# Gate/up expert by expert in a mixture-of-experts layer: split signals, split refills, earlier weight loads

## What is computed

```python
def hierarchical_moe(x, w_rg, b_rg, w_re, b_re, w_gate, w_up, w_down):
    ...  # gates: (tokens, 32), two nonzero entries in a row
    def per_seq(args):
        xi, gi = args
        hid = jax.nn.silu(jnp.einsum('sd,edf->sef', xi, w_gate)) * jnp.einsum('sd,edf->sef', xi, w_up)
        return jnp.einsum('sef,se,efd->sd', hid, gi, w_down)
...
x = x + jnp.concatenate([y_ssm, y_att], axis=-1) @ w_out[l]
x = x + hierarchical_moe(rmsnorm(x, norm_ffn_w[l]), ...)   # w_gate, w_up: (32, 1024, 256), w_down: (32, 256, 1024)
```

## Time and profile before

| | us |
|---|---|
| median of 3 runs | 785.33 (783.24 to 787.1) |
| the profiled execution, its own time | 782.43 |
| its span in the profile | 780.8 |
| TensorE busy | 712.0 (91%) |
| mean DMA rate over the span | 192 GB/s |
| granted TensorE clock, mean | 0.958 of full speed |

### The profile page before, as it was taken

How to read it: one execution, slowest core, us unless ns; L and a number is a source line. 1 busy time by engine, 2 the same in 40 slices (tenths; PEclk the granted TensorE clock), 3 DMA queues, 4 the chain that set the end, 5 groups by cost and what they waited for, 6 DMA issues and landing times.

```text
span 780.8 us, 10344 instructions
## 1 busy us (share of the span) xinstructions
PE 712.0 (91%) x3818; PEld 473.9 (61%) x3818; DVE 378.6 (48%) x758; ACT 279.1 (36%) x647; POOL 145.4 (19%) x124
## 2 busy tenths in 40 slices
PE   5999999999999999999999999978999678788884
PEld 4877888788788888566566688863333223233321
DVE  6776877775877734666776543660211111111100
ACT  4844643544554454544654423211221111111200
POOL 3423332330320102001210132011212111111111
PEclk9999999999999999999999999959999889899988
DMA  8333322330303330600110089489999999999962
GB/s 276 81 109 108 94 56 80 96 106 3 108 15 95 95 98 24 216 1 1 56 55 1 1 297 425 193 320 397 394 397 407 395 409 414 404 411 407 371 242 40
DMA packets 44005, 150.28 MB, mean 192 GB/s; under 512 B 11540, under 2 KB 11632, under 8 KB 32176
## 3 DMA queue, kind: packets, MB, share of 16 engines
q1 hardware_dynamic: 38384, 134.61, 45.5%
q0 software_dynamic: 4688, 8.67, 4.5%
q10 hardware_dynamic: 880, 6.30, 2.0%
HBM read 145.09 MB, written 12.85 MB: 202 GB/s over the span
## 4 chain that ended last, share of the span: by engine, by line
PE 65%; SPq 13%; DMA 10%; DVE 6%; ACT 3%; issue 2%; POOL 0%; POOLq 0%; ACTq 0%; DVEq 0%
PE bank L1067 13%; PE bank L1069 12%; PE bank L1068 12%; SPq L363 9%; DMA s_gu<-in_w_expert_up_dram 7%; PE bank L1438 7%; SPq L379 4%; PE bank L1304 3%; PE bank L1276 2%; PE bank L1462 2%; PE bank L1290 2%; PE bank L1184 2%; PE bank L1280 1%; DMA s_raw<-in_w_in_dram 1%; DVE s_wl L257 1%
## 5 line engine op out<-in xcount | busy, mean ns | idle before, releaser
L1438 PE MATMUL bank<-s_gu,s_xgT 128*64 128x512 f32 x512 | 127.7, 656 | 35.9 <-DMA s_gu<-in_w_expert_up_dram 32.7
L1438 PEld LDWEIGHTS bank<-s_gu,s_xgT 128*64 128x64 f32 x512 | 43.2, 151 | 118.4 <-issue 114.7
L257 DVE TENSOR_TENSOR s_wl<-s_raw,s_wh 128x512 fp32r<-128x512 f32 x84 | 86.7, 1070 | 25.5 <-ACT s_wh L747 25.2
L747 ACT ACTIVATE s_wh<-s_raw 128x512 fp32r<-128x512 f32 x120 | 74.0, 630 | 38.9 <-PE bank L1069 18.4
L257 POOL TENSOR_TENSOR s_wl<-s_raw,s_wh 128x512 fp32r<-128x512 f32 x36 | 54.7, 1532 | 130.7 <-ACT s_wh L747 130.0
L1067 PE MATMUL bank<-s_wh,s_hTh 128*128 128x512 f32 x192 | 78.7, 410 | 0.0
L1069 PE MATMUL bank<-s_wh,s_hTl 128*128 128x512 f32 x192 | 75.0, 391 | 0.0
L1068 PE MATMUL bank<-s_wl,s_hTh 128*128 128x512 f32 x192 | 74.8, 389 | 0.0
L1964 DVE COPY s_hidT<-bank 128x256 f32<-128x256 f32 x16 | 6.8, 424 | 121.8 <-PE bank L1447 121.8
L1462 PE MATMUL bank<-s_dn,s_hidT 128*64 128x512 f32 x256 | 58.5, 598 | 1.0 <-DVE s_hidT L1964 1.0
L998 ACT ACTIVATE s_sg<-bank,s_slot_scale 128x256 f32<-128x256 f32 x16 | 7.6, 474 | 141.6 <-PE bank L1438 141.6
(11 more groups left out here) (269 smaller groups left out, 1311.8 us busy)
## 6 DMA issues: line engine op xcount, KB each, us to landing
s_dn<-in_w_expert_down_dram SPq DMA_DIRECT2D x30, 1024.0 KB, 23.4
s_gu<-in_w_expert_gate_dram SPq DMA_DIRECT2D x28, 1024.0 KB
s_gu<-in_w_expert_up_dram SPq DMA_DIRECT2D x28, 1024.0 KB
s_raw<-in_w_in_dram SPq DMA_DIRECT2D x88, 256.0 KB, 3.4
s_raw<-in_w_out_dram SPq DMA_DIRECT2D x32, 256.0 KB, 3.3
s_xin<-in_x_dram SPq DMA_DIRECT2D x4, 512.0 KB, 5.6
s_zs<-in_x_dram SPq DMA_DIRECT2D x1, 2048.0 KB, 10.5
s_gu<-in_w_expert_gate_dram ACTq DMA_DIRECT2D x2, 1024.0 KB
```

The lines of the kernel that those rows point to most:

```text
L257: eng.tensor_tensor(low, full, high.bitcast(F32), ALU.subtract).then_inc(sem(f"{what}_low_{low_engine(what, i)}"), 1)
L747: act.activation(wh[:, i % HL, :], raw[:, i % RAW, :], ACT.Copy).then_inc(sem("w_high"), 1)
L1438: last = pe.matmul(ps[j][r, :].rearrange("p (w f) -> p w f", w=2), m["xgT"][:, j, k, r], gu[:, half, :, k, :], start=(k == 0), stop=(k == ...
```

## The change

Three things are edited.

1. In `gate_up` the loops are exchanged: all eight matmuls of half 0, then all eight of half 1. Each half waits for a semaphore of its own (`gu_in{b}_0`, `gu_in{b}_1`, two transfers each), and half 0's last matmul raises a new semaphore, `gate_up_half`.
2. The refill of a buffer is issued in two steps: parts 0 and 1 after `gate_up_half`, parts 2 and 3 after `gate_up_done`. The last pair is loaded like the others, and `load_last_gate_up` is gone.
3. Of pair 1's weights, parts 2, 0 and 3 are issued during the last output pass, each after `slot_used` says that tile 1, 3 or 5 of that pass is done (and the square of chunk 2), ahead of the stores of chunk 3. Part 1 follows the end of the pass, and parts 0 and 1 of pair 2 come right behind it; before, they waited for the first gather (`xg_in0`). The down weights of pair 3 now stand directly behind that wait.

```diff
--- before.py
+++ after.py
@@ -333,14 +333,13 @@
                 low_made(sp, "w", i - RAW)
             sp.dma_start(raw[:, i % RAW, :], slot_source(i)).then_inc(sem(f"raw_in{i % RAW}"), 16)
 
-        def gate_up_in(eng, p, r4):
+        def gate_up_in(eng, p, r4, half):
 
             if isinstance(p, int):
-                if p < NPAIR - 1:
-                    eng.wait_ge(sem(f"gu_in{p % NGU}"), 64 * (p // NGU + 1))
+                eng.wait_ge(sem(f"gu_in{p % NGU}_{half}"), 32 * (p // NGU + 1))
                 return m[f"gu{p % NGU}"]
             b = r4 % 2
-            eng.wait_ge(sem(f"gu_in{b}"), (p - b) * 32 + 64 * (len(range(b, NPAIR - 1, NGU)) + 1 - NPAIR // 2))
+            eng.wait_ge(sem(f"gu_in{b}_{half}"), (p - b) * 16 + 32 * (len(range(b, NPAIR, NGU)) + 1 - NPAIR // 2))
             return m[f"gu{b}"]
 
         def down_in(eng, p, r4):
@@ -360,17 +359,7 @@
                     if 2 * half + which not in parts:
                         continue
                     src = w[0][bass.ds(e + half * NPAIR, 1)].rearrange("e (p k) f -> p (e k f)", p=P)
-                    sp.dma_start(m[f"gu{b}"][:, half, which, :, :].rearrange("p k f -> p (k f)"), src).then_inc(sem(f"gu_in{b}"), 16)
-
-        def load_last_gate_up(sp):
-
-            p = NPAIR - 1
-            for part in range(2):
-                rows = slice(part * KC // 2, (part + 1) * KC // 2)
-                for half in range(2):
-                    for which, w in ((0, w_expert_gate), (1, w_expert_up)):
-                        src = w[0][p + half * NPAIR].rearrange("(p k) f -> p k f", p=P)[:, rows, :]
-                        sp.dma_start(m[f"gu{p % NGU}"][:, half, which, rows, :], src).then_inc(sem(f"gu_last{part}"), 16)
+                    sp.dma_start(m[f"gu{b}"][:, half, which, :, :].rearrange("p k f -> p (k f)"), src).then_inc(sem(f"gu_in{b}_{half}"), 16)
 
         def load_down(sp, p, b, wrap=False):
             e = p % NPAIR if wrap else p
@@ -456,33 +445,40 @@
                 low_made(sp, "w", i)
             load_down(sp, 1, 1)
 
+            def slots_free(k):
+                sp.wait_ge(sem("slot_used"), (NSLOT // KC - 1) * (KC - 1) + k + 1)
+
             for c in range(TC):
+                if c == TC - 1:
+                    sp.wait_ge(sem("f_squared"), TC - 1)
+                    slots_free(1)
+                    load_gate_up(sp, 1, 1, parts=(2,))
+                    slots_free(3)
+                    load_gate_up(sp, 1, 1, parts=(0,))
+                    slots_free(5)
+                    load_gate_up(sp, 1, 1, parts=(3,))
                 sp.wait_ge(sem("residual_added"), 12 + c + 1)
                 sp.dma_start(x2_dram[c * P:(c + 1) * P, :], zs[:, c, :]).then_inc(sem("x2_out"), 16)
                 sp.dma_start(out[c * P:(c + 1) * P, :], zs[:, c, :]).then_inc(sem("out_stored"), 16)
             sp.wait_ge(sem("pass_done"), N_END)
-            sp.wait_ge(sem("f_squared"), TC - 1)
-            load_gate_up(sp, 1, 1)
+            load_gate_up(sp, 1, 1, parts=(1,))
+            load_gate_up(sp, 2, 2, parts=(0, 1))
             sp.wait_ge(sem("xg_in0"), 16)
-            load_gate_up(sp, 2, 2, parts=(0, 1))
 
             sp.wait_ge(sem("x2_out"), 16 * TC)
             sp.wait_ge(sem("out_stored"), 16 * TC)
             sp.wait_ge(sem("f_squared"), TC)
             sp.wait_ge(sem("x2_transposed"), 2 * TC)
             load_down(sp, 3, 3)
-            sp.wait_ge(sem("gate_up_done"), 1)
-            load_gate_up(sp, 3, 0)
-            for p in range(4, NPAIR + 1):
+            for p in range(3, NPAIR + 1):
                 if p > 4:
                     sp.wait_ge(sem("down_done"), p - NDN)
                     load_down(sp, p - 1, (p - 1) % NDN)
                 if p < NPAIR:
+                    sp.wait_ge(sem("gate_up_half"), p - NGU + 1)
+                    load_gate_up(sp, p, p % NGU, parts=(0, 1))
                     sp.wait_ge(sem("gate_up_done"), p - NGU + 1)
-                if p < NPAIR - 1:
-                    load_gate_up(sp, p, p % NGU)
-                elif p < NPAIR:
-                    load_last_gate_up(sp)
+                    load_gate_up(sp, p, p % NGU, parts=(2, 3))
             sp.wait_ge(sem("most_known"), 1)
             over_cap = sp.value_load(most_i[0:1, 0:1])
             with sp.If(over_cap > CAP):
@@ -1429,14 +1425,14 @@
                 pe.wait_ge(sem("xgT_dve"), p + 1)
                 if not isinstance(p, int) or p >= 2:
                     pe.wait_ge(sem("hid_done"), p - 1)
-                gu = gate_up_in(pe, p, r4)
-                for k in range(KC):
-                    if isinstance(p, int) and p == NPAIR - 1 and k % (KC // 2) == 0:
-                        pe.wait_ge(sem(f"gu_last{2 * k // KC}"), 64)
-                    for half in range(2):
-                        r = slice(half * CAP, (half + 1) * CAP)
+                for half in range(2):
+                    gu = gate_up_in(pe, p, r4, half)
+                    r = slice(half * CAP, (half + 1) * CAP)
+                    for k in range(KC):
                         last = pe.matmul(ps[j][r, :].rearrange("p (w f) -> p w f", w=2), m["xgT"][:, j, k, r],
                                          gu[:, half, :, k, :], start=(k == 0), stop=(k == KC - 1))
+                    if half == 0:
+                        last.then_inc(sem("gate_up_half"), 1)
                 last.then_inc(sem("gate_up_done"), 1)
 
             def hid_transpose(p):
```

## The result

The changed kernel takes **819.11 us** (median of 4 runs, 815.93 to 821.22) against 785.09 us before. The ratio is 1.0429, with a 95% interval of 1.0403 to 1.0456: 34 us slower. The prediction said 781.7 us. The profiled execution took 821.22 us, its span 819.6.

The account below looks back on a forecast made before the run. In the experts the 16 DMA engines were taken as the limit, TensorE having slack. Terms -1.0 - 0.3 - 2.8 + 0.5 = -3.6 on 782.43 gave 778.8, plus 2.9 for the median, 781.7 us; range 774 to 850.

Parts of the forecast that it names:

- What bounds the kernel: In the experts the 16 DMA engines are the limit; TensorE has slack, 32.7 us idle there for gate/up transfers.
- a pair's period above 15 us: Sign, in the pairs at 550 to 590 us, that the forecast would be wrong.
- How a gate_up gets 7 us: In gate_up both array halves work side by side, taking 6.89 us; one after another, 32 records would take 13.8 us.
- Whether eight fit is a matter of the queue ahead of the array: In gate_up, some 20 of 32 records wait, half 0 has 16, so half 1's first would be in the queue.
- The halves run one after the other: Rival, chance 0.33: gate_up takes 13.8 us, TensorE bounds every pair, 848 us; 834 if one matmul more passes.
- Passing of a few only: Rival, chance 0.11: half of the overlap kept, gate_up takes 10.3 us, 792 us in all.
- (a): Last output pass: three of pair 1's 1 MB transfers issued early, shortening the first gather's backlog; -1.0 us with pair 2's.
- (b): Pair 2's parts 0 and 1 issued right behind pair 1's, not at 524.21; shares the -1.0 us (0 to -2).
- (c): Chunk 3 stores behind three new waits on SP land 1 us later, pair 3's down weights come earlier: nothing.
- (d): Refills by halves: half 0 ends hardly ahead of half 1, so -0.3 us (0 to -4).
- (e): Tail: half 0 of gate_up(14) starts before all parts land, -2.8 us (0 to -4); half 1's lag +0.5.
- The early transfers count in full: Rival, chance 0.06: all DMA idle time between 494 and 538, estimated 13 us, and the tail come back: 770 us.

Follow-up runs that it names:

- experiment 6: The kernel before with only the early loads of pairs 1 and 2 added: 783.55 us, ratio 0.9969.
- experiment 1: The changed kernel with the alternating order of matmuls put back, early loads and refills by halves kept: 783.36 us, ratio 0.9984.
- experiment 7: The changed kernel with alternating matmuls, except pair 14, which runs half 0's eight, then half 1's, each behind its own wait: 785.09 us, ratio 0.9996.
- experiment 12: The kernel before's alternating order with early loads, only the refills of pairs 14 and 15 split by rows, all others whole: 784.19 us, ratio 0.999.

## Why the prediction was wrong, step by step

**What bounds the kernel** was read rightly, and so was the point from which the order of the matmuls decides. `gate_up` could grow by 2.9 us until TensorE became the bound; it grew by 5.18, and (5.18 - 2.9) x 16 = 36 us is near the 34 measured. The prediction's own sign of being wrong, a pair's period above 15 us, came too: it is 16.98.

**How a gate_up gets 7 us** was right on the mechanism: two halves of the array side by side, and half 1 passing waiting matmuls of half 0. **The step that failed** is the sentence "Whether eight fit is a matter of the queue ahead of the array". It took the some 20 records of the earlier trace rows (16 by the weight loads that had not started in that trace) for the distance over which a matmul can be picked. These are two things. In the changed kernel some 17 records were waiting, and half 1 got past three. The earlier trace rows showed passing over one matmul and no more; the step from one to eight had no row, and it carried a chance of 0.50.

**The rivals.** The one that happened lies between two. "The halves run one after the other" had 13.8 us for a `gate_up` and 848 us, or 834 with one matmul more at the border; what was mis-sized is the overlap there, four records and not two. Four records are 1.72 us, so 12.07 us and, by its own sum, 526.4 + 281 + 9.3 = 816.7 of span and 821 us. "Passing of a few only" had the right kind, a reach of a few, with half of the overlap kept (10.3 us, 792 us). It is a quarter: a run of sixteen records has one border, at which four pass. Working out "a few" as a number of records per border would have given the time.

**The rule of the Trainium skill** that the prediction weighed ("TensorE: Matmul & The Clock Gate", Part 3, "The mechanism": matmuls start and end in program order) isn't what the trace shows: half 1's first record starts with three of half 0's still waiting. But for a run of eight its result was nearer to the time than mine.

**(a) and (b), the early loads, -1.0.** Right in size (-1.25 us alone, by the medians), and right that the full buffers take the rest back: experiment 6 shows 6.8 us of standstill. The gather is about 1 us shorter over all kernels with early loads, though not in the trace of experiment 6.

**(c)** was not tested by itself. The stores of chunk 3 are issued 9.3 us behind those of chunk 2 in both traces, and experiment 1 leaves no room for a loss.

**(d), the refills by halves, -0.3.** Right for halves that alternate, as there is nothing to gain: in run 1's kernel the first refill is issued at 537.22, 8.9 us after the first `gate_up` starts, against 8.5 before. In the changed kernel half 0 ends 5.2 us ahead of half 1, but the `gate_up` around it is as much longer, and the first refill is issued 9.1 us after the start. What frees a part at half time, the refills by rows, was worth nothing without the early loads (786.46 us) and up to 4.7 us with them (778.84 against 783.55 us, timed apart).

**(e), the tail, -2.8, and its lag.** Wrong, and with both halves at work too, as far as a split by rows can stand for it. The step asked when pair 14's weights land, and not what is late next. The last of pair 15's weights land 233.4 or 233.5 us after the first `gate_up` starts, whether pair 14 is early or not (experiment 7), and splitting pair 14 by rows, which brought it forward by 5.9 us, brought the end nothing (experiment 12).

**The early transfers count in full (770)** didn't happen; with the two refills behind them by rows, 5.2 of its 15 us came.

## What to carry to other kernels

Count how far apart, in instructions, two matmuls stand that are to run side by side on different columns of the array, and let no more than three matmul records stand between the partners: one or two float32 matmuls in a row were free here, four cost 1.9 us of 7, eight cost 5.2. A buffer that two interleaved users share is freed early by splitting it along the loop that both run through, not between the users. And before crediting a transfer that is brought forward, look for the next wait of the same stream, at the front (is a buffer free for what follows?) and at the end (what lands last?).

## What the hardware showed that was not expected

- Matmuls on different column halves pass each other over exactly three waiting records at both widths that were run (12.07 us with 32 records of 512 columns, 13.00 with 64 of 256), although some 17 stand in front of the array.
- At the same DMA share of 1.02, refills in transfers of 512 KB moved 391 and 395 GB/s, and those of 1 MB 403 GB/s.
- The end of the weight stream is thin. In the kernel with (14, 15) by rows the last weights are waited for until 760.04, while the DMA share is 0.13 to 0.19 from 757 on, as much as two or three of the 16 engines at work would give. Whether some engines are late, and what makes them so, stays open.
